# A hybrid decoder layer on one core: the experts' slot table summed on TensorE, and the pooled half of the samples' output projection done within the prompt attention

## What is computed

```python
hs = hs + jnp.concatenate([pool_o, attn_o], axis=-1) @ w_out[l]
hs = hs + hier_moe(rms_norm(hs, norm_ffn_g[l]), *moe_args)
...
def hier_moe(h, ...):
    g_sel = jnp.argmax(g_logits, axis=-1)             # 1 of 4 groups
    top_w, top_i = lax.top_k(jax.nn.softmax(e_in, axis=-1), EXPERT_TOPK)   # 2 of its 8 experts
    eid = (g_sel[:, None] * EXPERTS_PER_GROUP + top_i).reshape(-1)
    ...                                               # tokens sorted by expert, in blocks
        xb = x_pad[toks]
        return (jax.nn.silu(xb @ w_gate[e]) * (xb @ w_up[e])) @ w_down[e]
    y = jnp.zeros((N, D), jnp.float32).at[st].add(out[dest].astype(jnp.float32) * sw[:, None])
```

## Time and profile before

| | us |
|---|---|
| median of 3 runs | 1315.68 |
| lowest, highest | 1315.27, 1321.46 |
| profiled execution: its own time | 1309.84 |
| profiled execution: its span | 1308.0 |
| PE busy, share of the span | 1086.6, 83% |
| DVE busy, share | 630.8, 48% |
| ACT busy, share | 350.9, 27% |
| POOL busy, share | 210.8, 16% |
| mean granted clock of TensorE | 0.913 |

### The profile page before, as it was taken

The page is one execution under the profiler, slowest core; times in us unless marked ns, Lnnn a source line. Parts: engine busy times, 40 slices in busy tenths (PEclk is TensorE's granted clock), DMA queues, the critical chain, the costliest instruction groups (busy, mean ns, idle before and its releaser), DMA issues.

```text
span 1308.0 us, 16451 instructions
## 1 busy us (share of the span) xinstructions
PE 1086.6 (83%) x6188; PEld 739.7 (57%) x6188; DVE 630.8 (48%) x1433; ACT 350.9 (27%) x759; POOL 210.8 (16%) x272
## 2 busy tenths in 40 slices
PE   4999989998740399999789799729999999999940
PEld 2654424543420167777567655518777887778820
DVE  2225469999999977766652153040111111111128
ACT  1234441111330235555444133210111111111113
POOL 1522126543210000000000023110000000000032
PEclk9999999999885589999889789959999999999975
DMA  6510000100880201110101274319999999999847
GB/s 200 190 43 9 8 21 0 33 5 2 230 317 31 96 16 50 49 49 34 49 17 49 98 313 156 115 37 387 344 335 351 337 334 333 339 342 347 311 144 290
DMA packets 55483, 209.62 MB, mean 160 GB/s; under 512 B 11582, under 2 KB 13454, under 8 KB 45173
## 3 DMA queue, kind: packets, MB, share of 16 engines
q1 hardware_dynamic: 38271, 142.25, 30.3%
q0 software_dynamic: 13408, 53.80, 11.7%
q10 hardware_dynamic: 3742, 12.75, 2.5%
HBM read 171.35 MB, written 37.54 MB: 160 GB/s over the span
## 4 chain that ended last, share of the span: by engine, by line
PE 62%; DVE 28%; DMA 4%; issue 3%; ACT 2%; POOL 1%; POOLq 0%; SPq 0%; ACTq 0%; DVEq 0%; PEldq 0%
PE ps L1417 18%; DVE mem L1924 12%; PE ps L1423 9%; PE ps L1276 7%; PE ps L1069 5%; PE ps L1024 3%; PE ps L1057 3%; PE ps L1227 3%; PE ps L1410 2%; PE ps L1238 2%; PE ps L1250 2%; PE ps L1287 2%; DVE mem L2217 1%; ACT mem L1493 1%; DVE mem L1953 1%
## 5 line engine op out<-in xcount | busy, mean ns | idle before, releaser
L1493 ACT ACTIVATE mem<-ps 128x512 f32<-128x512 f32 (+10 forms) x376 | 171.7, 495 | 387.3 <-PE ps L1238 72.2
L1417 PEld LDWEIGHTS ps<-mem 128*128 128x128 f32 x2048 | 236.8, 194 | 16.7 <-issue 16.7
L1417 PE MATMUL ps<-mem 128*128 128x96 f32 x2048 | 236.2, 277 | 0.8 <-DVE mem L2315 0.8
L1924 DVE TENSOR_SCALAR_CACHE_REDUCE mem<-mem 128x384 bf16<-128x384 f32 (+2 forms) x182 | 199.6, 1140 | 0.0
L1276 PE MATMUL ps<-mem 128*128 128x256 f32 (+1 forms) x576 | 132.7, 384 | 6.4 <-DVE mem L2170 2.8
L1276 PEld LDWEIGHTS ps<-mem 128*128 128x128 f32 (+1 forms) x576 | 104.5, 187 | 25.9 <-DVE mem L2170 4.6
L1423 PE MATMUL ps<-mem 128*96 128x512 f32 x256 | 117.6, 602 | 0.9 <-DVE mem L2307 0.8
L2307 DVE TENSOR_TENSOR mem<-mem,ps 128x192 f32<-128x192 f32 x32 | 11.4, 355 | 220.9 <-ACT mem L1795 220.9
L1238 PE MATMUL ps<-mem 128*128 128x128 f32 x288 | 48.4, 298 | 55.7 <-ACT mem L1702 54.3
L1795 ACT ACTIVATE mem<-ps 128x192 f32<-128x192 f32 x32 | 10.6, 330 | 265.0 <-PE ps L1417 265.0
L962 POOL DMA_INDIRECT mem<-xn_rows,mem x32 | 29.0, 906 | 323.1 <-PE ps L1410 315.7
(11 more groups left out here) (273 smaller groups left out, 1348.0 us busy)
## 6 DMA issues: line engine op xcount, KB each, us to landing
mem<-in_expert_w_gate SPq DMA_DIRECT2D x32, 1024.0 KB, 5.5
mem<-in_expert_w_up SPq DMA_DIRECT2D x32, 1024.0 KB, 8.6
mem<-in_expert_w_down SPq DMA_DIRECT2D x32, 1024.0 KB, 10.7
expert_rows<-mem ACTq DMA_DIRECT2D x32, 384.0 KB, 8.0
expert_rows<-mem POOLq DMA_DIRECT2D x1, 9216.0 KB, 29.1
mem<-in_x_prompt SPq DMA_DIRECT2D x16, 512.0 KB, 4.2
mem<-in_w_in SPq DMA_DIRECT2D x3, 2048.0 KB, 10.3
h_rows<-mem SPq DMA_DIRECT2D x8, 512.0 KB, 2.6
```

The lines of the kernel that those rows point to most:

```text
L1417: ins = mm(ps[:, 2 + s, j * CAP:(j + 1) * CAP], wgu[w][:, j // 2, k, (j % 2) * P:(j % 2 + 1) * P], xgT[:, s, k, :], start=(k == 0), stop=( ...
L1493: return fn(out, in_, ACT.Copy, scale=scale)
L1924: v.tensor_scalar(bufs[a % 3][0:R, 0:w], sc, mid[:, a:a + 1], None, ALU.is_ge, ALU.add, accum_out=cnt[:, a:a + 1]).then_inc(step, 1)
```

## The change

1. The 64 sample rows get their residual and the pooled half of the output projection earlier. A new buffer `hbS`, in columns 0 to 255 of each of `mixP`'s four parts, takes `x_sample`, which SP loads behind tile 6's store. Four steps ("OP", NT, 0) to 3, of 4 products instead of 8, are put among the last tail tasks of tile 7.
2. After the samples' attention only its half is left: ("OP", NT, 4) and 5, of 512 columns each, in two banks (7 and 4).
3. ACT computes a square root of a constant before it waits for these, so that the table of the root is loaded then.
4. The slot table is a sum of products: a one-hot row of the slot (96 columns) against the expert's one-hot row times the token number. For the prompt, 16 such products are summed behind pair 2's outputs ("slots"); for tile 8 there are two (SL); DVE adds both and writes the table. Scatters, load and `behind` and `first` are gone.
5. POOL's drain comes behind its last gather of V, and POOL waits for `slots_ready` instead of for all engines.
6. DVE's `destinations()` is moved from ahead of the first expert to behind the fourth. Its operations are the same.
7. The constants get 96 columns more (`slot`, 0 to 95).

```diff
+        slot_hot = [mixP[:, n, 256:1024].rearrange("p (i s) -> p i s", s=CAP) for n in range(2)]
+        token_hot = [mixP[:, 2, 256 * (n + 1):256 * (n + 2)].rearrange("p (i e) -> p i e", e=NE) for n in range(2)]
+        slotP = mixP[0:CAP, 3, 256:256 + NE]
+        slot_sum = mixP[0:CAP, 3, 288:288 + NE]
+        slot_hot_s = [mixP[0:SR, 3, 320 + CAP * n:320 + CAP * (n + 1)] for n in range(2)]
+        token_hot_s = [mixP[0:SR, 3, 512 + NE * n:512 + NE * (n + 1)] for n in range(2)]
         def row_buffer(lo):
...
         def tail_tasks(i):
-            return ([("OT", i)] if i < NT else []) + [("OP", i, q) for q in range(4)] + [
-                ("SQ", i), ("NM", i), ("XR", i, 0), ("XR", i, 1), ("LG", i)] + ([("RK", i)] if i == NT else [])
+            return [("OP", i, 4), ("OP", i, 5), ("SQ", i), ("NM", i), ("XR", i, 0), ("XR", i, 1), ("LG", i), ("RK", i), ("SL", i)]
...
+        def part_of(t):
+            return "PT0" if t == ("OP", NT, 5) else "M"
+        def last_op(i):
+            return ("OP", i, 3) if i < NT else ("OP", NT, 5)
...
         tasks += [("OP", i - 1, 3), ("SQ", i - 1), ("OT", i), ("OP", i, 0), ("NM", i - 1), ("OP", i, 1), ("XR", i - 1, 0),
-                  ("OP", i, 2), ("XR", i - 1, 1), ("OP", i, 3), ("LG", i - 1), ("SQ", i), ("NM", i),
-                  ("XR", i, 0), ("XR", i, 1), ("LG", i)]
+                  ("OP", i, 2), ("XR", i - 1, 1), ("OP", i, 3), ("LG", i - 1), ("SQ", i), ("OP", NT, 0), ("NM", i), ("OP", NT, 1),
+                  ("XR", i, 0), ("OP", NT, 2), ("XR", i, 1), ("OP", NT, 3), ("LG", i)]
...
                 tk("rank")
+            if p == 2:
+                tk("slots")
...
+                    sp.dma_start(hbS, rowsof(x_rows, i).rearrange("t (q n) -> t q n", q=4)).then_inc(xr_in[s], 16)
+                else:
+                    sp.dma_start(hb[0:r, s, :], rowsof(x_rows, i)).then_inc(xr_in[s], 16)
...
-            residual(NT)
             weights(1, 1)
...
-            for i in range(TILES):
-                scatter(i)
-            pool.wait_ge(slots_out, 16 * 2 * TILES)
-            pool.dma_start(slot_tok[0:CAP, 0:NE].bitcast(I32), slot_dram[0:NE * CAP, 0:1].rearrange("(c p) k -> p (c k)", p=CAP),
-                           allow_slow_non_contiguous=True).then_inc(slots_in, 16)
-            pool.wait_ge(slots_in, 16)
+            pool.drain().then_inc(phase2, 1)
+            pool.wait_ge(slots_ready, 1)
             tiles_out(pool, x2_out, TILES)
-            pool.drain().then_inc(phase2, 1)
-            pool.wait_ge(phase2, 4)
...
-                        else:
-                            lhs = mixS[:, k - 4, :] if i == NT else mixA[:, k - 4, :]
-                        ins = mm(ps[0:r, 7, 0:256], lhs, wout[:, k, 256 * t[2]:256 * t[2] + 256], start=(k == 0), stop=(k == 7))
+                    if t[2] >= 4:
+                        half = slice(512 * (t[2] - 4), 512 * (t[2] - 3))
+                        for k in range(4):
+                            ins = mm(ps[0:r, 7 if t[2] == 4 else 4, :], mixS[:, k, :], wout[:, 4 + k, half], start=(k == 0), stop=(k == 3))
+                        ins.then_inc(filled["2b" + part_of(t)], 1)
+                        return
+                    last = 3 if i == NT else 7
+                    for k in range(last + 1):
+                        lhs = mixP[:, k, tok] if k < 4 else mixA[:, k - 4, :]
+                        ins = mm(ps[0:r, 7, 0:256], lhs, wout[:, k, 256 * t[2]:256 * t[2] + 256], start=(k == 0), stop=(k == last))
                 elif kind == "XR":
                     pe.wait_ge(x2_ready, i + 1)
...
+                elif kind == "SL":
+                    pe.wait_ge(hot_ready, 2)
+                    for n in range(2):
+                        ins = mm(ps[0:CAP, 7, 0:NE], slot_hot_s[n], token_hot_s[n], start=(n == 0), stop=(n == 1))
...
                     mm(flat8, const("ones"), PRE8[:, :, :].rearrange("p i e -> p (i e)"), start=False, stop=True)\
                         .then_inc(filled[f"2cTK{part}"], 1)
+                if p == 2:
+                    part = tk_use["slots"]
+                    pe.wait_ge(hot_ready, 1)
+                    claim(pe, "2c", f"TK{part}", "slots")
+                    for i in range(NT):
+                        for n in range(2):
+                            ins = mm(ps[0:CAP, 5 + part, 0:NE], slot_hot[n][:, i, :], token_hot[n][:, i, :],
+                                     start=(i == 0 and n == 0), stop=(i == NT - 1 and n == 1))
+                    ins.then_inc(filled[f"2cTK{part}"], 1)
             settle(pe, "2c")
             for t in tail_tasks(NT):
...
-                    copied(act, "2b", "M", ("OP", i, 3))
                     if i >= 2:
                         act.wait_ge(x2_out[s], 16 * (i // 2))
                         take(act, "2b", "M", ("XR", i - 2, 1))
-                    fn(x2[0:r, s, :], hb[0:r, s, :], ACT.Square, accum_out=ssq2[0:r, i:i + 1]).then_inc(ssq2_ready, 1)
+                    if i == NT:
+                        fn(std2[0:r, i:i + 1], const("z", r), ACT.Sqrt)
+                        copied(act, "2b", "M", ("OP", i, 4))
+                    copied(act, "2b", part_of(last_op(i)), last_op(i))
+                    h = hbS if i == NT else hb[0:r, s, :]
+                    sq_out = x2[0:r, s, :].rearrange("p (q n) -> p q n", q=4) if i == NT else x2[0:r, s, :]
+                    fn(sq_out, h, ACT.Square, accum_out=ssq2[0:r, i:i + 1]).then_inc(ssq2_ready, 1)
...
+                for n in range(2):
+                    ins = v.tensor_scalar(slot_hot_s[n], const("slot", r), RK[0:r, i, n:n + 1], None, ALU.is_equal)
+                ins.then_inc(hot_ready, 1)
                 v.tensor_tensor(ASUM[0:r, :], ASUM[0:r, :], A[0:r, :], ALU.add).then_inc(ASUM_ready, 1)
-                dve.wait_ge(ASUM_ready, 2)
-                link(v.tensor_scalar(FF[0:r, :], RK[0:r, i, :], float(CAP), float(NBLK * CAP + 2 * NTOK), ALU.is_ge, ALU.mult))
-                link(v.tensor_tensor(FF[0:r, :], FF[0:r, :], RK[0:r, i, :], ALU.add))
-                link(v.scalar_tensor_tensor(out=FF[0:r, :], in0=EF[0:r, i, :], scalar=float(CAP), in1=FF[0:r, :],
-                                            op0=ALU.mult, op1=ALU.add))
-                link(v.tensor_tensor(FF[0:r, :], FF[0:r, :], behind[0:r, i, :], ALU.min))
-                v.tensor_copy(first[0:r, i, :], FF[0:r, :]).then_inc(first_ready, 1)
+            def slots(i):
+                take(dve, "2b", "M", ("SL", i))
+                v.tensor_tensor(slot_sum, ps[0:CAP, 7, 0:NE], slotP, ALU.add).then_inc(emptied["2bM"], 1)
+                copied(dve, "2b", "M", ("SL", i))
+                v.tensor_copy(slot_tok[0:CAP, 0:NE], slot_sum).then_inc(slots_ready, 1)
...
-                link(v.tensor_scalar(two, RK[:, 0:NT, :], float(CAP), float(NBLK * CAP + 2 * NTOK), ALU.is_ge, ALU.mult))
-                link(v.tensor_tensor(two, two, RK[:, 0:NT, :], ALU.add))
-                link(v.scalar_tensor_tensor(out=two, in0=EF[:, 0:NT, :], scalar=float(CAP), in1=two, op0=ALU.mult, op1=ALU.add))
-                link(v.tensor_tensor(two, two, behind[:, 0:NT, :], ALU.min))
-                v.tensor_copy(first[:, 0:NT, :], two).then_inc(first_ready, NT)
+                for n in range(2):
+                    v.tensor_tensor(token_hot[n], OH8[:, n], const("tokid")[:, 0:NT].unsqueeze(2).broadcast_to([P, NT, NE]), ALU.mult)
+                    ins = v.tensor_tensor(slot_hot[n], RK[:, 0:NT, n].unsqueeze(2).broadcast_to([P, NT, CAP]),
+                                          const("slot").unsqueeze(1).broadcast_to([P, NT, CAP]), ALU.is_equal)
+                ins.then_inc(hot_ready, 1)
+            def keep_slots():
+                part = tk_use["slots"]
+                take(dve, "2c", f"TK{part}", "slots")
+                v.tensor_copy(slotP, ps[0:CAP, 5 + part, 0:NE]).then_inc(emptied[f"2cTK{part}"], 1)
             def weigh_prompt():
...
                     take(dve, "2b", "M", t)
...
+                    slots(i)
+                    weigh(i)
...
+                link(v.tensor_scalar(ovT[:, :], const("iota"), float(CAP), float(CAP), ALU.mult, ALU.add))
...
             keep_xgT(0, 0)
             experts(0)
+            destinations()
             with dve.Fori(1, NE // WSLOTS - 1) as q:
                 experts(q)
             experts(NE // WSLOTS - 1, last=True)
```

127 lines of the change are left out of this document (65 added, 62 removed).

## The result

| | before | after |
|---|---|---|
| median of the runs compared, us | 1318.33 (1315.27 to 1321.46, 4 runs) | 1297.83 (1296.70 to 1300.01, 4 runs) |
| profiled execution, us | 1309.84, span 1308.0 | 1298.67, span 1296.8 |
| mean granted clock, profiled | 0.913 | 0.921 |

The changed kernel takes 0.9839 of the time before, with a 95% interval of 0.9817 to 0.9861: it is 20.5 us faster. The two profiled spans, though, differ by 11.2 us, almost exactly the sum of the prediction.

A forecast was written before the change was run, and what follows sets the result against it. It took a chain of waits on small transfers, then experts bound by PE, as the limit. Its terms summed to -11.4 us, from a median of 1315.7 to 1304.3 us, range 1300 to 1312.5.

The forecast's parts named there:

- small ones, up to LG 6: More constants ahead of the first weights, +0.1 us, and two operations for `behind` gone from DVE, -0.4 us.
- pooled half into the prompt attention: Four product steps among tile 7's tail tasks, handed on through one bank with nothing overlapping: +5.7 us.
- prompt part of the slot table: 32 short PE instructions on the path between pair 2's output turn and pair 3's probability turns: +2.9 us (1.9 to 3.9).
- attention half: End of the samples' attention: 8 products of 512 columns back to back replace four round trips through bank 7, -9.3 us.
- root's table: Tail of tile 8: idle ACT loads the square root's table during the products, taking it off the path, -1.3 us.
- slot table at the end: From ranks to first gather: two scatters, their landing, the table's load and POOL's drain go from the path, -11.0 us.
- destinations and the rest: DVE's 8.64 us chain does not fit its 6.79 us idle behind the fourth expert, so PE stalls: +1.9 us.
- Rival 1: PE's clock falls in the new steps at the end of the prompt attention, leaving -2.5 us or +3 to +5; chance 0.22.
- Rival 2: POOL's 2.92 and 0.8 us belong to the first wait behind its transfers and come again: -7.7 us; chance 0.1.
- Rivals 3 and 4: First expert finds something else late, -5.4 us, chance 0.05; clock stays half in the experts, +6.6 us, chance 0.04.

The follow-up runs named there:

- e4: The changed kernel with the destinations ahead of the first expert again: 1297.78 us, ratio 0.9837 to the kernel before.
- e14: The changed kernel with 32 memsets keeping POOL busy where the scatters had stood, without any transfer: 1298.10 us, ratio 0.983 to the kernel before.
- e1: The kernel before, run again without any edit: 1316.28 us over 12 runs, ratio 0.9985.
- e5: The kernel before without the 16 scatters of the prompt's tokens: 1306.06 us, ratio 0.9899.
- e8: The changed kernel with 16 unread scatters put ahead of POOL's last two value loads: 1310.84 us, ratio 0.9927 to the kernel before.
- e2: The kernel before with only the samples' pooled half of the projection moved and the root's table loaded early: 1315.42 us, ratio 0.9964.
- e6: The changed kernel with 16 scatters put back where the old ones stood, into rows nobody reads: 1308.61 us, ratio 0.9917 to the kernel before.
- e10: The changed kernel with the samples' pooled half moved into two idle PE stretches of tile 6: 1288.28 us, ratio 0.976 to the kernel before.
- e12: The changed kernel with 16 gathers of 128 rows where the old scatters stood: 1311.57 us, ratio 0.9944 to the kernel before.
- e9: The changed kernel with the prompt's slot table products moved behind the attention half, into a bank of their own: 1294.15 us, ratio 0.981 to the kernel before.
- e11: The changed kernel with both the edits of e9 and e10: 1285.45 us, ratio 0.9746 to the kernel before.
- e7: The changed kernel with 8 unread scatters, one for each tile, put back where the old ones stood: 1302.36 us, ratio 0.9862 to the kernel before.
- e13: The changed kernel with 16 gathers of only 16 rows each where the old scatters stood: 1313.77 us, ratio 0.9948 to the kernel before.

## Why the prediction was wrong on the time and right on the span

From profiled span to profiled span the terms came out as follows; each measured value is the growth of the distance between two marks of the path.

| term | forecast | measured | marks |
|---|---|---|---|
| small ones, up to LG 6 | -0.3 | +0.7 | PE starts LG 6, 735.16 and 735.89 |
| pooled half into the prompt attention | +5.7 | +5.7 | DVE takes LG 7, 746.21 and 752.65 |
| up to pair 3's maximum | 0 | -1.3 | 816.33 and 821.49 |
| prompt part of the slot table | +2.9 | +4.8 | values of pair 3, 825.01 and 835.01 |
| attention half | -9.3 | -9.6 | its last sum ends, 847.84 and 848.23 |
| root's table | -1.3 | -1.4 | ranks, 861.02 and 859.97 |
| slot table at the end | -11.0 | -11.3 | first gather, 874.89 and 862.53 |
| gather to first product | 0 | -0.6 | 882.15 and 869.15 |
| destinations and the rest | +1.9 | +1.8 | end of the span |
| sum | -11.4 | -11.2 | 1308.0 and 1296.8 |

That the sum comes within 0.2 is in part luck: four rows miss by 0.6 to 1.9 and cancel. The -1.3 ahead of pair 3's maximum goes with the clock in the first pair of samples, 0.59 and 0.57 in the two stretches from 762 to 770 before and 1.00 in both now; the prediction had nothing there. The +0.7 up to LG 6 is not traced. And +4.8 for the slot table is one execution's number; with the +2.4 of e4 and e14 the sum would have been -13.6.

**The step that failed** is the last one of the sum: "That run was 5.8 us under the median of the three others, 1315.7; on the median I expect 1304.3". It took the profiled execution for a usual one with a constant put on top, and subtracted the same 11.4 from either. The offset was no constant: the changed kernel's median lies 0.8 below its profiled execution (1297.83 and 1298.67) instead of 5.9 above it, and these 5.9 are nearly all of the 6.5 us between 1304.3 and 1297.8. What lay between the usual execution and the profiled one was a part of what the change removes. In a usual execution of before the 16 scatters of the prompt hold up PE, ACT and DVE (e1), and in the profiled one they happened not to. The sum priced the two scatters of the samples, whose landing stood in the chain, and gave the 16 others no price, since POOL had nothing else to do and nobody waited for them. e5 to e8 give their price: 4.6 us for 8, 10.8 to 13.4 for 16. The gain in the span, 11.2, and the hold-up that is gone, 10.6 (e1's maximum against the first one's), make 21.8; measured were 20.5. One gap is left in this account: the profiles that show the hold-up in a kernel with the old scatters are of e1's slower group and of e2; no run of before near 1316 was profiled. That both groups of e5 lie 13.4 lower speaks for the same hold-up in both.

**The slot term** missed by the clock, not by the work. At full clock the 32 instructions take 2.83 (e4, e6, e8, e10, e12, e14) or 2.90 (e9, e11), as forecast, and the term is +2.4 (e4, e14). In the profile of after the clock fell to half among them, which made them 3.97 and the turns behind them 1.05 longer: +4.8. Rival 1, the clock falling in the new steps, was looked for at 738 to 752, where it stayed full; in this one execution it came in another new step. The Trainium skill (TensorE: Matmul & The Clock Gate, LDWEIGHTS) would have given 2.6 for this term; in e4 and e14 the turns start 2.66 behind the first of the 32, which agrees.

**The root's table** came at -1.4, by the row and not by the page: Square and root now stand 1.18 apart (848.33 and 849.51), and no row shows the drain that the Trainium skill (ScalarE: Activation LUTs, What ACT_TABLE_LOAD costs) adds to a switch.

**The destinations** stalled PE by 1.48 in the fifth expert as forecast (1.9), in one gap. What the prediction did not say is that the old place was not free any more either: with the table's load gone, the chain stands in the way of the first expert's copy there, and e4 shows the two places to be equal within the noise.

**Rival 2** is settled by the first gather, 0.4 us after the start of DVE's cast (862.09 and 862.53): the 2.92 and 0.8 had belonged to the drain at that place. Rivals 3 and 4 did not come: the first gather is 12.4 us earlier and the first product 13.0, and behind the gap the clock is 1.00.

**Left open.** Why the issue of indirect transfers slows other engines, and why not in every execution (the first profile of before, one run of e7). I can say that ACT and DVE start late behind PE, that PE has gaps within its own stream, and that in e1, e2, e6 and e12 this stream is whole again 2.8 to 3.2 us behind the end of POOL's last issue. A load of 16 KB of instructions that lands at 817.8 in the first profile of before lands at 827.8 in e1, but there PE's stream is whole from 826.79 on, and in e6 such a load lands at 824.6, 9 us ahead of the late maximum; so its landing is not what ends the hold-up. Nor do I know why the runs of before fall into two groups, near 1316 and near 1321: those of e5, without the prompt's scatters, do so too (1302 to 1304 and 1308 to 1309). The granted clock of the slower group is lower each time, by 0.002 to 0.006. An estimate for e1's two groups: a mean clock lower by 0.004 is 0.008 of the 1318 us, or 11 us, more at half clock, worth at most 5.5 us, about the distance of the groups; what lowers the clock is open.

## What to carry to other kernels

When the profiled execution lies well off the other runs (5.8 us here), ask which part of the program ran otherwise in it, and whether the change touches that part. An engine that is idle is not free to issue transfers on: a row of indirect transfers from POOL cost 0.6 to 1.0 us each here, though nobody waited for them, while the same stretch of plain work on POOL cost nothing. A block of products that must stand somewhere belongs into a stretch where PE waits anyway: there it cost next to nothing (PE's next step began 0.5 later, 648.88 and 648.38) and the clock behind it was higher.

## What the runs showed of the hardware that was not expected

- Sixteen indirect transfers issued by POOL one behind the other (every 1.15 to 1.28 us) lengthened the kernel by 10.8 us (scatters), 13.8 us (gathers) and 16.0 us (gathers of 16 rows); 32 memsets over 18 us by 0.3 us.
- During them ACT began up to 6 us after the end of the PE work that it waited for (823.4 and 829.36 in e13), DVE 9 us (817.9 and 826.95 in e1).
- Short products with 96 columns of weights and 32 of data, PE busy throughout: the granted clock went from 1.00 to 0.50 among them in the profile of after (828 us) and stayed at 1.00 in those of e4 and e14, in the same place behind the same work. The clock of a stretch this short is a matter of the execution, and one profile doesn't settle it.
- Filling two idle stretches of PE (8.6 and 4.6 us) with 7.2 us of products gave 9.5 us, 3.8 more than these products had cost elsewhere; 2.1 of them lie in the stretch behind the idle times, where the clock was 0.83 and 0.91 instead of 0.74 twice.
